# Block attention of a fused two-block kernel: keys, queries and the first four heads' probabilities turned by full-width VectorE transposes and a block exchange through device memory

## What is computed

```
q, k, v = split(h @ w_in, 3)                      # 8 heads of 128
q = partial_rope(q, pos) * Dh ** -0.5             # the first 32 columns of each head are rotated
k = partial_rope(k, pos)
s = where(causal, q @ k.T, NEG);  p = exp(s - max(s));  l = sum(p)
o = (p @ v + b * sum(v)) / (l + 256 b)            # 256 tokens are one block: the "selected" part is only the constant b
return o @ w_out
```

## Time and profile before

| | us |
|---|---|
| median of 3 runs | 1101.28 (1101.17 to 1101.91) |
| profiled execution, its own time | 1102.08 |
| its span, first to last instruction | 1100.1 |
| TensorE busy | 1090.8 (99%) |
| VectorE busy | 841.8 (77%) |
| ScalarE busy | 663.4 (60%) |
| GpSimd busy | 196.5 (18%) |

### The profile page before, as it was taken

The page is one execution under the profiler, slowest core; times in us unless marked ns, Lnnn a source line. Parts: engine busy times, 40 slices in busy tenths (PEclk is TensorE's granted clock), DMA queues, the critical chain, the costliest instruction groups (busy, mean ns, idle before and its releaser), DMA issues.

```text
span 1100.1 us, 12969 instructions
## 1 busy us (share of the span) xinstructions
PE 1090.8 (99%) x5095; PEld 906.6 (82%) x5095; DVE 841.8 (77%) x956; ACT 663.4 (60%) x811; POOL 196.5 (18%) x135
## 2 busy tenths in 40 slices
PE   9999999999999999999999999999999999999997
PEld 7788888888888887888888888888888888888886
DVE  5786668776569988778538569999677976799964
ACT  6646566654767664654588366576465646655651
POOL 1434700000343420000013000004306000000430
PEclk9999999999999999999999999999999999999999
DMA  9645444545555479555534546559855244554970
GB/s 355 244 166 196 128 174 151 218 172 190 179 193 207 167 201 329 213 223 181 193 125 160 204 172 238 180 165 259 298 195 217 102 167 170 202 181 162 251 240 38
DMA packets 31800, 214.60 MB, mean 195 GB/s; under 512 B 3768, under 2 KB 3936, under 8 KB 6912
## 3 DMA queue, kind: packets, MB, share of 16 engines
q1 hardware_dynamic: 28320, 195.61, 48.7%
q0 software_dynamic: 3424, 18.23, 7.7%
HBM read 212.77 MB, written 1.05 MB: 194 GB/s over the span
## 4 chain that ended last, share of the span: by engine, by line
PE 94%; DVE 2%; DMA 2%; ACT 1%; issue 1%; SPq 0%; DVEq 0%; ACTq 0%
PE ps L789 77%; PE ps L1318 3%; PE aux L862 3%; PE aux L1266 2%; PE ps L1266 2%; DMA raw<-in_wstream 2%; PE ps L1320 1%; PE ps L905 1%; PE aux L1111 1%; DVE Wl L2044 1%; PE aux L1355 1%; ACT Wh L1484 1%; PE aux L1096 1%; PE ps L982 0%; PE aux L1342 0%
## 5 line engine op out<-in xcount | busy, mean ns | idle before, releaser
L789 PE MATMUL ps<-Wh,xT 128*128 128x512 f32 x1792 | 559.9, 391 | 0.0
L2044 DVE TENSOR_TENSOR Wl<-raw,Wh 128x2048 fp32r<-128x2048 f32 x188 | 434.9, 2323 | 130.3 <-ACT Wh L1484 128.7
L1484 ACT ACTIVATE Wh<-raw 128x2048 fp32r<-128x2048 f32 x192 | 366.1, 1914 | 171.7 <-PE ps L789 157.4
L789 PEld LDWEIGHTS ps<-Wh,xT 128*128 128x128 f32 x1792 | 336.4, 188 | 69.8 <-issue 0.3
L789 PE MATMUL ps<-Wl,xT 128*128 128x512 f32 x896 | 348.6, 389 | 0.0
L789 PEld LDWEIGHTS ps<-Wl,xT 128*128 128x128 f32 x896 | 168.3, 188 | 34.1
L2648 DVE STREAM_TRANSPOSE htmp<-held 32x512 f32<-32x512 f32 x128 | 89.9, 702 | 2.5
L789 PE MATMUL ps<-Wh,hTh 128*128 128x512 f32 x192 | 74.8, 389 | 0.0
L789 PE MATMUL ps<-Wh,hTl 128*128 128x512 f32 x192 | 74.7, 389 | 0.0
L789 PE MATMUL ps<-Wl,hTh 128*128 128x512 f32 x192 | 74.7, 389 | 0.0
L693 POOL DMA_DIRECT2D raw<-in_wstream x12 | 10.7, 892 | 236.8 <-DVE Wl L2044 236.8
(11 more groups left out here) (419 smaller groups left out, 1545.8 us busy)
## 6 DMA issues: line engine op xcount, KB each, us to landing
raw<-in_wstream SPq DMA_DIRECT2D x182, 1024.0 KB, 4.8
raw<-in_wstream POOLq DMA_DIRECT2D x12, 1024.0 KB, 8.6
grow<-in_post_gains POOLq DMA_DIRECT2D x4, 512.0 KB, 5.5
grow<-in_b_gate POOLq DMA_DIRECT2D x6, 256.0 KB, 3.5
mrows<-in_mem SPq DMA_DIRECT2D x2, 512.0 KB, 5.6
raw<-in_wstream SPq DMA_DIRECT2D x2, 512.0 KB, 6.9
x<-in_x SPq DMA_DIRECT2D x1, 1024.0 KB, 13.9
out<-x SPq DMA_DIRECT2D x4, 256.0 KB, 2.0
```

Of the source, the lines that this page charges most:

```text
L789: mm = nc.tensor.matmul(ps[2 * pair + t][:, :], a[:, kt, t * P:(t + 1) * P], w[:, slot, j, :], start=(first and j == 0 and q == 0), stop=( ...
L1484: nc.scalar.activation(split_view(Wh, g), weight_view(raw, g), ACT.Copy).then_inc(hi_ready, 1)
L2044: nc.vector.tensor_tensor(split_view(Wl, g), weight_view(raw, g), split_view(Wh, g).bitcast(F32), ALU.subtract).then_inc(lo_ready, 1)
```

## The change

ScalarE now drains queries and keys in another layout, in which for each group c of 32 head columns the blocks (head, token half) of 32 columns lie side by side; the keys' factor of 128 ** -0.5 is applied in this drain (`x4_keys`, a small VectorE instruction makes it). After the rotation SyncE writes each row tile to device memory in four transfers of 32 partitions (`blocks_out`) and reads it back in one transfer with the 32-blocks exchanged between partition groups (`blocks_in`). One VectorE transpose over 128 partitions and 1024 columns (`turn_moved`) then gives the turned operand of four heads. TensorE's key transposes, ScalarE's copies of them and VectorE's 32-partition query transposes are gone. The probabilities of heads 0 to 3 take the other order: one VectorE transpose over 128 x 2048 (`turn_first_probs`), out to device memory and back, and TensorE reads `turned_p` with 32-column pieces (`moba_first_out`). Heads 4 to 7 keep the way through TensorE for their probabilities.

```diff
+                if g == P0["moba2"] + 7:
+                    rows_out("q0", BQ[:, 0, :, :, :, :], "bq_rot", 1)
+                elif g == P0["moba2"] + 8:
+                    rows_in("q0")
+                    rows_out("k0", BK[:, 0, :, :, :, :], "bk_rot", 1)
+                elif g == P0["moba2"] + 9:
+                    rows_in("k0")
+                    rows_out("q1", BQ[:, 1, :, :, :, :], "bq_rot", 2)
+                elif g == P0["moba2"] + 10:
+                    rows_in("q1")
+                elif g == P0["moba2"] + 11:
+                    rows_out("k1", BK[:, 1, :, :, :, :], "bk_rot", 2)
+                    sp.wait_ge(sem("bqk_turned"), 1)
+                    rows_in("k1")
+                    blocks_out("p", blocks_p[:, :, :, :].rearrange("p c b j -> p c (b j)"), "p_blocks", 1)
+                elif g == P0["moba2"] + 12:
+                    blocks_in("p", turned_p[:, :, :, :, :, :].rearrange("p q h t k j -> p q (h t k j)"))
                 if not ADDED[g]:
                     sp.wait_ge(lo_ready, g + 1 - RING)
...
+            def blocks_out(name, blocks, ready, count):
+
+                sp.wait_ge(sem(ready), count)
+                for q in range(4):
+                    sp.dma_start(line[name][:, :, q, :].rearrange("c i e -> i c e"), blocks[32 * q:32 * q + 32, :, :])\
+                        .then_inc(sem("line_out"), 16)
+
+            def blocks_in(name, dst):
+
+                n = LINES.index(name)
+                sp.wait_ge(sem("line_out"), 64 * n + 64)
+                if n:
+                    sp.wait_ge(sem("line_in"), 16 * n)
+                sp.dma_start(dst, line[name].rearrange("c i q e -> (c i) q e")).then_inc(sem("line_in"), 16)
...
-            turn_keys(0)
             product("moba3", (xTh, xTl))
-            pe.wait_ge(sem("bq_turned"), 1)
-            wait_operand("bkT0", range(2))
+            pe.wait_ge(sem("bqk_turned"), 2)
...
             product("moba4", (xTh, xTl))
-            turn_keys(1)
-            for h in range(4):
-                turn_probs("bpT", h, bprob, "b_prob")
...
             wait_drained(pe, "moba4", 1)
+            pe.wait_ge(sem("line_in"), 16 * len(line))
             for h in range(4):
-                moba_out(h)
+                moba_first_out(h)
...
+            def turn_moved(name, dst):
+
+                dve.wait_ge(sem("line_in"), 16 * list(line).index(name) + 16)
+                nc.vector.transpose(dst.rearrange("p h (t q j) -> p (h t) q j", q=4, j=32),
+                                    moved[name][:, :, :, :].rearrange("p q b j -> p b q j")).then_inc(sem("bqk_turned"), 1)
+
+            unit("moba2")
+            turn_moved("q0", bqT[:, 0:4, :])
+            turn_moved("k0", bkT[:, 0:4, :])
...
-            unit("moba3", lambda: turn_queries(1, 8, 16), *(lambda h=h: masked_max(h) for h in range(4)),
-                 *(lambda h=h: moba_probs(h) for h in range(4)))
...
+            unit("moba3", None, lambda: turn_moved("q1", bqT[:, 4:8, :]), *(lambda h=h: masked_max(h) for h in range(4)),
+                 *(lambda h=h: moba_probs(h) for h in range(4)), turn_first_probs, lambda: turn_moved("k1", bkT[:, 4:8, :]))
+            unit("moba4")
```

More of the change, by code:

```diff
@@ L1431, in _, with moba_values, moba_first_out @@
             product("moba5", (xTh, xTl), before={1: second_scores})
+            def moba_values(h, ks):
+                return BV[:, h // 4, ks, (h % 4) * HD:(h % 4 + 1) * HD]
+            def moba_first_out(h):
+                o = open_aux("boT", h)
+                for ks in range(2):
+                    for t0, t1 in ((0, 1), (1, 2)) if h == 3 and ks else ((0, 2),):
+                        mm = nc.tensor.matmul(o[:, t0 * P:t1 * P], moba_values(h, ks),
+                                              turned_p[:, :, h, t0:t1, ks, :].rearrange("p q t j -> p t q j"),
+                                              start=(ks == 0), stop=(ks == 1), skip_group_check=True)
+                done(mm, "boT", h)
             def moba_out(h):
                 wait_read(pe, "bpT", h)
-                attend("boT", h, lambda ks: BV[:, h // 4, ks, (h % 4) * HD:(h % 4 + 1) * HD], bpT)
+                attend("boT", h, lambda ks: moba_values(h, ks), bpT)
             wait_drained(pe, "moba4", 1)
+            pe.wait_ge(sem("line_in"), 16 * len(line))
             for h in range(4):
-                moba_out(h)
+                moba_first_out(h)
             def second_heads():
@@ L1992, in _ @@
                 moba_exps(h)
-            def second_turned():
-                bk_turned(1)
-                rows("moba4", lambda t: BV[:, 0, t, :], "x4")()
-            unit("moba4", second_turned)
+            unit("moba4", rows("moba4", lambda t: BV[:, 0, t, :], "x4"))
             def moba_probs(hs):
@@ L2726, in _, with turn_first_probs @@
             unit("moba0")
+            dve.wait_ge(sem("norm_rstd"), NORMS["x4"])
+            nc.vector.tensor_scalar(S("x4_keys"), S("x4_rstd"), HD ** -0.5, None, ALU.mult).then_inc(sem("x4_scaled"), 1)
             unit("moba1")
-            def turn_queries(j, first, last):
-                dve.wait_ge(sem("bq_rot"), j + 1)
-                src = BQ[:, j, :, :].rearrange("p t (h d) -> p t h d", d=HD)
-                dst = bqT[:, 4 * j:4 * j + 4, :].rearrange("p h (t j) -> p t h j", j=P)
-                for ab in range(first, last):
-                    a, b = 32 * (ab // 4), 32 * (ab % 4)
-                    i = nc.vector.transpose(dst[b:b + 32, :, :, a:a + 32], src[a:a + 32, :, :, b:b + 32])
-                if last == 16:
-                    i.then_inc(sem("bq_turned"), 1)
-            turn_queries(0, 0, 8)
-            unit("moba2", lambda: turn_queries(0, 8, 16))
-            turn_queries(1, 0, 8)
+            def turn_moved(name, dst):
[5 more added lines that the diff above has]
+            turn_moved("k0", bkT[:, 0:4, :])
+            def turn_first_probs():
+                dve.wait_ge(sem("b_prob"), 8)
+                nc.vector.transpose(blocks_p[:, :, :, :].rearrange("p c b j -> p b c j"),
+                                    bprob[:, :, :, :].rearrange("p h t (k c j) -> p (h t k) c j", c=4, j=32))\
+                    .then_inc(sem("p_blocks"), 1)
             def masked_max(h):
```

64 lines of the change are left out of this document (34 added, 30 removed).

## The result

The changed kernel takes 1105.35 us (median of 6 runs, 1104.36 to 1107.09), the kernel before 1101.36 (6 runs, 1101.17 to 1101.91): a ratio of 1.0036, 95% interval [1.0025, 1.0047]. It is slower by 4.0 us. The forecast was 1102.0, no difference that can be measured; the time lies inside the stated range and outside the forecast's own (1099.9 to 1103.5). The profiled execution took 1105.05 us with a span of 1103.2, 3.0 us more than the one before. The six runs of the changed kernel spread over 2.7 us, those of the kernel before over 0.7.

The account below looks back on a forecast made before the run. TensorE, 99% busy, and VectorE's chain to the projection bound it almost level. TensorE's 3.50 us go to waiting; 863.9 + 30.8 puts the projection at 894.7, 0.7 later: 1102.8 profiled, median 1102.0, range 1098.3 to 1106.5.

Parts of the forecast that it names:

- S: Start of VectorE's first maximum, 863.81 before the change; forecast at 863.9, between 861.8 and 865.4, chance 0.42.
- dearer stores: Exchange stores costing 4.4 us a tile like small packets: S 870.8, about 1111 us; chance 0.09 including late probabilities.
- What TensorE gives back: TensorE's removed transposes: 0.88 us for the first eight, 2.62 for the 24 behind moba4, together 3.50 us at most.
- VectorE's list: VectorE's work from first maximum to output projection: 12.3 us replace 11.7, so the projection starts at S + 30.8.
- I add up the transfers, in the order in which SyncE issues them, as one queue: Exchanges and loads on SyncE's queue: three times store 2.1, load 2.6, read back 1.3, 18.0 us from 843.8.
- the ledger: The sum of queued transfers from 843.8: data end at 861.8, q1 lands at 862.5, is turned by 863.7.
- On the way k0 lands at 856.7 ... Both are covered: Keys ahead of the scores: turned by 857.9, before the scores' 859.35; split 154 follows until 860.1; no cost.
- The rival of half-rate stores: Stores from 32 partitions take 2.6 us or more a tile: S 865.4, median 1103.5; chance 0.23.
- The fast queue: Rival: stores flow at the load's rate and transfers overlap; S 860.2, 3.0 us gained, 1098.3; chance 0.20.
- The probabilities' return: Heads 0 to 3 read back by 888.5; TensorE waits 2.0 us from 886.5, costing only beyond 890.8.
- The rotation behind split 153: GpSimd's rotation of the second queries, held up by VectorE's split: 2.1 us later, at 854.3, covered at the store price.
- the third round trip: The second queries' q1 out to device memory and back, behind q0 and k0: lands at 862.5 and sets S.

Follow-up runs that it names:

- e_both: Changed kernel with q0, k0, q1 exchanged ahead of load 155, later exchanges ahead of their loads, and q1's transpose behind the probabilities': 1100.58 us, ratio 0.9991 to before.
- m_stores: Kernel before, with 512 KiB stores in several forms and read backs added behind its last output, each awaited alone: four 32-partition stores 3.6 us, one 128-partition store 2.6.
- e_late: Changed kernel with VectorE's transpose of q1 moved behind that of the probabilities, plus two buffer waits: 1101.54 us, ratio 1.0000 to the kernel before.
- e_p_only: Kernel before with only the probabilities of heads 0 to 3 exchanged through device memory: 1103.69 us, ratio 1.0017.
- e_second_lock: Changed kernel with q0, k0, q1 exchanged ahead of load 155 and later exchanges ahead of loads; q0's transpose stays behind split 153: 1101.3 us, ratio 0.9997 to before.
- e_first: Changed kernel with SyncE issuing q0's and k0's trips ahead of load 155, load 155 still ahead of q1: 1104.35 us, ratio 1.0025 to the kernel before.

## What the prediction had right, and the step that failed

The time lies inside the stated range, but S at 866.45 lies outside the 861.8 to 865.4 on which the forecast rests. The range covers it because its high end was drawn for dearer stores, which isn't quite what happened: the number is in part luck. Of the 3.35 us between the forecast median and the measured one, 2.25 lie between the profiled executions (1102.8 forecast, 1105.05 measured); the rest is where the two profiled executions stand against their medians, 0.8 above and 0.3 below.

**What TensorE gives back** (3.50 us) was right. From the first to the second scores TensorE takes 18.98 us in e_both (858.71 to 877.69), without a wait, and 21.66 in the kernel before (860.23 to 881.89): 2.68 us less for the 24 transposes, 2.62 forecast. The eight in front are worth 0.88, which is how much earlier e_both reaches the first scores with the profiles lined up (842.64 against 843.28).

**VectorE's list** was right. The projection was forecast at S + 30.8 and starts at S + 30.7 (897.15 less 866.45); the wide transposes take 1.20 to 1.25 and 2.31 us where 1.2 and 2.25 were estimated from the 32-partition rows. So 128 partitions cost no more than 32 here.

**The step that failed** is "I add up the transfers, in the order in which SyncE issues them, as one queue". It gave S = 863.9; the profile has 866.45, 2.55 us later, and the projection is 2.45 later than forecast. From the first store of `q0` to the landing of `q1` the ledger had 22.05 us (840.45 to 862.5), and it took 24.85 (840.41 to 865.26), 2.8 more. Two parts of this are seen. The stores flow for about 2.5 us per tile (m_stores, in an empty queue), not 2.1: 1.2 us for three tiles, an estimate, as the flow of a store beside loads wasn't measured by itself. The other 1.6 are put down to what the ledger left out: a leg begins only when the one before has landed, and in those gaps the flow falls to 55 to 191 GB/s, while at other times a later transfer takes its share from an earlier one, as load 157 and `q1`'s stores do from the keys' read back. Which of the two carries more of the 1.6 was not separated, and e_late shows that the same order of transfers can come out 1.7 us shorter at one read back.

**"On the way k0 lands at 856.7 ... Both are covered"** was wrong for the same reason. `k0` landed at 860.25, and TensorE waited 2.21 us ahead of the scores. This wait didn't set the end: `q1`, turned by 866.5, did.

**The rival of half-rate stores** (2.6 us or more a tile, 1103.5) was the nearest in size: 2.5 us were measured. Its reason isn't borne out. The Trainium skill (SBUF — State Buffer, "Door 1: The DMA port swizzle (why [64,N] ≈ [32,N])") has 189 GB/s from 32 partitions against 328. Here the four stores flow at 190 to 270 and the single one at 400 to 419, but four stores over 128 partitions were no faster (3.9 us). That speaks for the split, with SyncE's 1.79 us for four issues, and against the reach of 32 partitions; no run compares one store of each. The fast queue, the rival on the faster side, was wrong for this kernel: transfers overlap, but what one gained another lost.

**The probabilities' return** was forecast at 888.5, with a cover up to 890.8. It came at 892.5: 2.5 us later for S, and 1.5 for stores and read back that share with loads. TensorE's wait for it was 2.08 us where 2.0 was forecast, and that agreement is luck: TensorE too arrived 4.0 us later, at 890.54 instead of 886.5, because of its wait of 2.21 us and its slower scores, so both sides had moved by the same amount. The cover had moved with S, so it still held in the changed kernel, where the projection waits for VectorE last. It would not hold for an S as forecast, which e_p_only shows: with S untouched this exchange alone cost 0.69 us at the projection and 2.0 in the median.

**The rotation behind split 153** was forecast to end at 854.3, 2.1 us later than before, and to be covered. It ended at 854.1, and the chain that ended last runs through it. But the read back of `k0` left SyncE's queue at 853.98 and the stores of `q1` were issued at 854.12, so it holds them by 0.14 us: covered nearly to the end. In e_second_lock, where the keys' read back is issued earlier, the hold-up of 2.0 us shows on the stores and still not on S.

So the mechanism was the forecast's, S through the third round trip, and the term that was mis-sized is the three round trips through the queue: 22.05 us forecast, 24.85 measured, which puts S 2.55 us later.

## What to carry to other kernels

A chain of round trips through a queue that was also loading wasn't a sum of flows here: measure one trip in the empty queue, expect more beside loads (6.8 us against 11.1 here), and place whatever has slack, loads and the waiting instruction, behind it. When work is taken from a busy engine and the time doesn't fall, look for the list of the engine it meets next; here moves of order in VectorE's and SyncE's lists (the exchanges ahead of the loads, the transpose of `q1`, split 158, the two copies), with no work removed, turned 4.0 us of loss into 2.5 us of gain. Each such move shows the next wait, so read the waits again after each.

## What the runs showed of the hardware beyond the forecast

**TensorE's clock after a wait.** In the changed kernel TensorE waited 2.21 us ahead of the scores, and they took 4.49 us instead of 2.79. The windows of the changed kernel over that stretch (start:end, length, busy time of PE, PEld, DVE, ACT, POOL, granted clock, DMA share, GB/s):

```profile
860.00:862.00 2.00, 0.41 (x2) 0.41 (x3) 1.71 (x2) 1.90 (x2) 1.73 (x4) 0.87 0.73 294
862.00:864.00 2.00, 2.00 (x8) 1.73 (x8) 1.71 (x1) 0.00 (x0) 2.00 (x1) 0.50 0.73 242
864.00:866.00 2.00, 2.00 (x13) 1.86 (x12) 0.72 (x1) 0.00 (x0) 0.89 (x3) 0.78 0.73 184
```

The granted clock fell from 1.00 (2.4 GHz) to 0.50 (1.2 GHz) behind the wait. It did so in e_first too, where TensorE waited 4.38 us and the first outputs took 6.76 us, and in e_second_lock (2.47 us, 5.39). It did not in e_p_only, where the wait was 3.26 us and the outputs took 3.71, nor at the changed kernel's own second wait (2.08 us, 3.71). So a wait of 2.1 to 4.4 us costs nothing more in some places and 1.7 to 3.1 us more in others; what decides is open. These are single profiled executions. The forecast had no term for it, and in the changed kernel it wasn't in the way: the 1.7 us lie beside VectorE's wait for `q1`, and the chain that ended last doesn't pass through the scores. In the profiled execution of e_first it was: the projection starts at 898.80, behind the outputs that took 6.76 us.

**VectorE and GpSimd hold each other up in both directions.** GpSimd's small instruction took 2.47 us instead of 0.46 beside a split on VectorE, and VectorE's smallest took 3.48 instead of 0.17 to 0.31 beside a split on GpSimd. The first direction was forecast, from the earlier trace rows; the second was not, and it was seen in one profiled execution.
